# One Trainium2 core, hybrid attention block: the order of the rotary embedding on ScalarE and VectorE, its operand buffers, and the shares of the merged heads

## The reference, cut to what matters

```python
qa = rope(qa.reshape(B, S, DSW_HEADS, HEAD_DIM), positions)   # 24 window heads of 64, in 3 groups
ka = rope(ka.reshape(B, S, DSW_HEADS, HEAD_DIM), positions)
for g, (win, dil) in enumerate(zip((128, 512, 2048), (1, 4, 16))):
    o_g, lse_g = dilated_window_attention(qa[:, :, sl], ka[:, :, sl], va[:, :, sl], win, dil)
alpha = jax.nn.softmax(jnp.stack(lses), axis=0)               # shares of the 3 groups, per row and head
ya = jnp.sum(alpha[..., None] * jnp.stack(outs), axis=0)
pa = (ya * jax.nn.silu(za)) @ w_proj_a

qd, kd = rope(qd, positions), rope(kd, positions)             # 8 differential heads, 2 x 64 each
yd = differential_attention(qd, kd, vd, lam)                  # softmax 1 - lam * softmax 2, dense
yd = rms_norm(yd, diff_subln) * (1.0 - lambda_init)
pb = (yd * jax.nn.silu(zd)) @ w_proj_b
y = (sigmoid(ga) * pa + sigmoid(gb) * pb) @ w_out
return x + gate * rms_norm(y, norm_post)

def rope(x, positions):   # x1, x2: the two halves of a head
    return concatenate([x1 * cos - x2 * sin, x2 * cos + x1 * sin])
```

## Time and profile before

| | |
|---|---|
| median of 3 runs | 929.48 us (927.55 to 931.8) |
| the profiled execution's own time | 928.42 us |
| its span, first to last instruction | 926.6 us |
| mean granted TensorE clock | 0.968 of full speed |
| busy: PE, PE weight load, DVE, ACT, POOL | 834.0, 696.0, 463.1, 358.1, 494.5 us |
| DMA | 94.77 MB in 89716 packets |

### The profile page before, as it was taken

The page is one execution under the profiler, slowest core; times in us unless marked ns, Lnnn a source line. Parts: engine busy times, 40 slices in busy tenths (PEclk is TensorE's granted clock), DMA queues, the critical chain, the costliest instruction groups (busy, mean ns, idle before and its releaser), DMA issues.

```text
span 926.6 us, 12694 instructions
## 1 busy us (share of the span) xinstructions
PE 834.0 (90%) x4622; PEld 696.0 (75%) x4622; DVE 463.1 (50%) x785; ACT 358.1 (39%) x777; POOL 494.5 (53%) x657
## 2 busy tenths in 40 slices
PE   1578799999999999998988879998899999999797
PEld 1568589888878788788767757875788777888697
DVE  2866377463534344322467767757756644212122
ACT  4233344444434343423434334543545632222311
POOL 2674445353464555335767674744546537638900
PEclk9989799999989999999988999999999999999899
DMA  9763372233233323222533222222122113323421
GB/s 256 212 185 92 108 267 81 69 91 104 68 104 103 103 69 108 83 96 80 170 96 92 87 74 69 80 80 69 58 69 65 50 46 114 114 69 123 150 73 65
DMA packets 89716, 94.77 MB, mean 102 GB/s; under 512 B 5133, under 2 KB 80950, under 8 KB 89526
## 3 DMA queue, kind: packets, MB, share of 16 engines
q1 hardware_dynamic: 89360, 93.54, 33.1%
q0 software_dynamic: 240, 0.39, 0.4%
q10 hardware_dynamic: 54, 0.02, 0.0%
HBM read 78.11 MB, written 5.34 MB: 90 GB/s over the span
## 4 chain that ended last, share of the span: by engine, by line
PE 42%; POOL 17%; DVE 13%; DMA 9%; ACT 7%; issue 7%; SPq 5%; ACTq 0%; DVEq 0%; POOLq 0%
PE proj L1465 29%; POOL w_lo L671 9%; PE proj L1548 4%; DMA rope_s<-rope_x 4%; POOL rope_x L696 3%; DVE rope_o L1076 3%; SPq L551 3%; PE score L1344 2%; DMA ada<-in_w_ada 2%; PE sums L1390 2%; PE turned L1361 2%; ACT w_hi L785 1%; DVE ada_sum L1006 1%; POOL h_lo L671 1%; PE score L1319 1%
## 5 line engine op out<-in xcount | busy, mean ns | idle before, releaser
L671 POOL TENSOR_TENSOR w_lo<-raw,w_hi 128x256 fp32r<-128x256 f32 x408 | 321.7, 820 | 245.0 <-ACT w_hi L785 244.9
L1465 PE MATMUL proj<-h_hi,w_hi 128*128 128x512 f32 x608 | 255.2, 420 | 10.2 <-POOL h_lo L681 7.9
L1465 PE MATMUL proj<-h_hi,w_lo 128*128 128x512 f32 x608 | 243.5, 401 | 0.0
L1465 PE MATMUL proj<-h_lo,w_hi 128*128 128x512 f32 x608 | 243.2, 400 | 0.0
L1465 PEld LDWEIGHTS proj<-h_hi,w_hi 128*128 128x128 f32 x608 | 117.8, 194 | 46.0 <-POOL h_lo L681 9.3
L1465 PEld LDWEIGHTS proj<-h_hi,w_lo 128*128 128x128 f32 x608 | 117.7, 194 | 26.7
L1465 PEld LDWEIGHTS proj<-h_lo,w_hi 128*128 128x128 f32 x608 | 118.1, 194 | 21.4
L785 ACT ACTIVATE w_hi<-raw 128x1024 fp32r<-128x1024 f32 x102 | 106.0, 1055 | 12.8 <-PE proj L1465 7.7
L696 POOL TENSOR_TENSOR rope_x<-rope_x,cos_t 128x512 f32<-128x512 f32 x36 | 53.9, 1496 | 84.8 <-DMA rope_s<-rope_x 84.4
L1139 DVE TENSOR_TENSOR at_lo<-turned,at_hi 128x512 fp32r<-128x512 f32 x64 | 44.1, 689 | 67.5 <-ACT at_hi L887 65.2
L1390 PE MATMUL sums<-v,at_hi 128*128 128x128 f32 (+1 forms) x256 | 63.1, 316 | 14.4 <-DVE at_lo L1139 14.2
(11 more groups left out here) (236 smaller groups left out, 1545.6 us busy)
## 6 DMA issues: line engine op xcount, KB each, us to landing
raw<-in_w_in SPq DMA_DIRECT2D x88, 512.0 KB, 3.6
rope_s<-rope_x SPq DMA_DIRECT2D x144, 64.0 KB, 2.3
ada<-in_w_ada SPq DMA_DIRECT2D x16, 512.0 KB, 6.2
zd<-in_w_ada SPq DMA_DIRECT2D x8, 512.0 KB, 4.9
raw<-in_w_proj_b SPq DMA_DIRECT2D x8, 512.0 KB, 3.4
raw<-in_w_out SPq DMA_DIRECT2D x8, 512.0 KB, 3.4
rows_in<-window_rows SPq DMA_DIRECT2D x4, 792.0 KB, 4.5
window_rows<-rows_out SPq DMA_DIRECT2D x4, 528.0 KB, 4.9
```

The lines of the kernel that those rows point to most:

```text
L671: ins = nc.gpsimd.tensor_tensor(lo[:, k, :], raw[:, n % RAW, k, :], hi.bitcast(F32)[:, k, :], ALU.subtract)
L1465: ins = mm(dst, left, right, start=k == 0 and n == 0, stop=k == nk - 1 and n == 2)
```

## The change

It has four parts. (1) On ScalarE, `rope_cut` moves behind `leave_bank`, `turned_hi` and `vt_hi` of its tick, and, but for the first four tiles, one tick on, to L + 3. (2) On VectorE, the sum of the rotation is a function of its own, `rope_add`, which runs at L + 3 behind the maxima and ahead of `join` (for the first four tiles directly behind the product with sin, as before); the rest of a tile is taken at L + 4. (3) The copy and the swapped copy have two buffers each, so `rope_copy` and the swap wait for the sum of the tile before the last. (4) The maxima and denominators of all rows are loaded by four small transfers into `mix_in` at tick 96, and `merge_weights` runs once, at tick 98, for all four quarters, with 32 columns per operation for 8; `mstat` and `mix_in` lie in memory of the early tensors.

```diff
+    add_tick = lambda t: rope_tick(t) + (t.u >= 4)
+    rope_add_at = by_tick([t for t in tiles if t.kind in "qk"], add_tick)
-    rope_lo_at = by_tick([t for t in tiles if t.kind in "qk"], lambda t: rope_tick(t) + 1)
+    rope_lo_at = by_tick([t for t in tiles if t.kind in "qk"], lambda t: add_tick(t) + 1)
...
-            return (zd[:, n, :], zd[:, 4 + n, :]) if n < 4 else (rope_x[:], rope_s[:])
+            return (zd[:, n, :], zd[:, 4 + n, :]) if n < 4 else (rope_x2[:, n % 2, :], rope_s2[:, n % 2, :])
...
                 sp.wait_ge(rope_copied, n + 1)
-                if n >= 5:
-                    sp.wait_ge(rope_done, n)
+                if n >= 6:
+                    sp.wait_ge(rope_done, n - 1)
...
                     if tt:
                         sp.wait_ge(merged_done, tt)
+                    else:
+                        for i in range(NT):
+                            sp.dma_start(mix_in[:, i, :, :], scratch[:, i * P:(i + 1) * P, 4 * HD:OW].rearrange("n p f -> p n f")).then_inc(mix_in_loaded, 16)
...
                     pool.wait_ge(rows_in_loaded, 16 * (tt + 1))
-                    pool.wait_ge(shares_done, tt + 1)
+                    pool.wait_ge(shares_done, 1)
...
                 act.wait_ge(proj_done, tile.u + 1)
-                if n >= 5:
-                    act.wait_ge(rope_done, n)
+                if n >= 6:
+                    act.wait_ge(rope_done, n - 1)
...
-                for tile in rope_at(t):
-                    rope_cut(tile)
                 for tile in tiles_done(t):
                     leave_bank(tile)
                 for s in trans_at(t):
                     turned_hi(s)
                 for tile in vt_at(t):
                     vt_hi(tile)
-                for tt in mix_at(t):
-                    act.wait_ge(mix_diff, tt + 1)
-                    nc.scalar.activation(mstat[:, 32:56], mstat[:, 8:32], ACT.Exp).then_inc(mix_exp_done, 1)
+                for tile in rope_add_at(t):
+                    rope_cut(tile)
+                if t == mix_tick[0]:
+                    act.wait_ge(mix_diff, 1)
+                    nc.scalar.activation(mstat[:, 4:7, :], mstat[:, 1:4, :], ACT.Exp).then_inc(mix_exp_done, 1)
...
+            def rope_add(tile):
+                n = rope_no[tile.u]
+                at, other = rope_place(tile)
                 dve.wait_ge(rope_sin_done, n + 1)
                 dve.wait_ge(rope_cos_done, n + 1)
...
+                for tile in rope_add_at(t):
+                    if tile.u >= 4:
+                        rope_add(tile)
                 for s in scores_at(t):
                     if s.group == 3:
                         join(s)
                 for tile in rope_at(t):
                     rope_turn(tile)
+                    if tile.u < 4:
+                        rope_add(tile)
...
-                for tt in mix_at(t):
-                    merge_weights(tt)
+                if t == mix_tick[0]:
+                    merge_weights()
```

More of the change, by code:

```diff
@@ L332, in build @@
         sin_t = sb("sin_t", [P, S], on=early)
-        rope_x = sb("rope_x", [P, S], on=early)
-        rope_s = sb("rope_s", [P, S], on=early)
+        rope_x2 = sb("rope_x", [P, 2, S], on=early)
+        rope_s2 = sb("rope_s", [P, 2, S], on=early)
+        rope_x, rope_s = rope_x2[:, 0, :], rope_s2[:, 0, :]
         rope_o = sb("rope_o", [P, S], on=early)
@@ L343, in build @@
         merged = sb("merged", [P, S], on=early)
+        mstat = sb("mstat", [P, 12, 32], on=early)
+        mix_in = sb("mix_in", [P, NT, N_WIN, 8], on=early)
         early.close()
@@ L371, in build @@
         rows_in_loaded = sem("rows_in_loaded")
+        mix_in_loaded = sem("mix_in_loaded")
         x_again = [sem(f"x_again{i}") for i in range(2)]
@@ L914, in _ @@
             act.wait_ge(angle_done, 1)
-            nc.scalar.activation(sin_t[:], rope_s[:], ACT.Sin).then_inc(act_sin, 1)
+            nc.scalar.activation(sin_t[:], rope_s, ACT.Sin).then_inc(act_sin, 1)
             act.wait_ge(angle_done, 2)
@@ L1043, in _ @@
             dve.wait_ge(pos_loaded, 16)
-            link(nc.vector.tensor_copy(rope_x[:], merged[:].bitcast(I32)))
-            link(ts_(rope_x[:], rope_x[:], rope_c[:, 0:1], None, ALU.mult))
-            link(ts_(rope_o[:], rope_x[:], float(1 / (2 * np.pi)), ROUND, ALU.mult, ALU.add))
+            link(nc.vector.tensor_copy(rope_x, merged[:].bitcast(I32)))
+            link(ts_(rope_x, rope_x, rope_c[:, 0:1], None, ALU.mult))
+            link(ts_(rope_o[:], rope_x, float(1 / (2 * np.pi)), ROUND, ALU.mult, ALU.add))
             link(ts_(rope_o[:], rope_o[:], ROUND, None, ALU.subtract))
             for part in TWO_PI:
[L1049 to L1053, removed]
+                link(stt(out=rope_x, in0=rope_o[:], scalar=-part, in1=rope_x, op0=ALU.mult, op1=ALU.add))
+            link(ts_(rope_x, rope_x, PI_BELOW, -PI_BELOW, ALU.min, ALU.max))
+            ts_(rope_s, rope_x, rope_c[:, 1:2], None, ALU.mult).then_inc(angle_done, 1)
+            link(stt(out=rope_x, in0=rope_x, scalar=-1.0, in1=rope_x, op0=ALU.mult, op1=ALU.max))
+            ts_(rope_o[:], rope_x, -1.0, float(np.pi / 2), ALU.mult, ALU.add).then_inc(angle_done, 1)
             dve.wait_ge(const_done, 2)
@@ L1187, in gate_head, with merge_weights @@
                     op0=ALU.mult, op1=ALU.mult).then_inc(t_read, 1)
[L1189 to L1194, removed]
-                link(tt_(m8(0), small(0, nb), small(1, nb), ALU.min))
-                link(tt_(m8(0), m8(0), small(2, nb), ALU.min))
+            def merge_weights():
+                dve.wait_ge(mix_in_loaded, 16 * NT)
+                small = lambda g, at: mix_in[:, :, 2 * g:2 * g + 2, at:at + 4]
+                m = lambda i: mstat[:, i, :].rearrange("p (t n h) -> p t n h", t=NT, n=2)
+                link(tt_(m(0), small(0, 0), small(1, 0), ALU.min))
+                link(tt_(m(0), m(0), small(2, 0), ALU.min))
                 for g in range(3):
-                    ins = tt_(m8(8 + 8 * g), m8(0), small(g, nb), ALU.subtract)
+                    ins = tt_(m(1 + g), m(0), small(g, 0), ALU.subtract)
                 ins.then_inc(mix_diff, 1)
-                dve.wait_ge(mix_exp_done, tt + 1)
+                dve.wait_ge(mix_exp_done, 1)
                 for g in range(3):
-                    link(tt_(m8(56 + 8 * g), m8(32 + 8 * g), small(g, den), ALU.mult))
-                link(tt_(m8(80), m8(56), m8(64), ALU.add))
-                link(tt_(m8(80), m8(80), m8(72), ALU.add))
-                link(nc.vector.reciprocal(m8(80), m8(80)))
+                    link(tt_(m(7 + g), m(4 + g), small(g, 4), ALU.mult))
+                flat = lambda i: mstat[:, i, :]
+                link(tt_(flat(10), flat(7), flat(8), ALU.add))
+                link(tt_(flat(10), flat(10), flat(9), ALU.add))
+                link(nc.vector.reciprocal(flat(10), flat(10)))
                 for g in range(3):
-                    ins = tt_(m8(32 + 8 * g), m8(32 + 8 * g), m8(80), ALU.mult)
+                    ins = tt_(flat(4 + g), flat(4 + g), flat(10), ALU.mult)
                 ins.then_inc(shares_done, 1)
```

3 lines of the change are left out of this document (1 added, 2 removed).

## The result

| | before | after |
|---|---|---|
| median | 930.64 us (4 runs, 927.55 to 932.12) | 901.12 us (4 runs, 896.14 to 901.99) |
| the profiled execution's own time, and its span | 928.42, 926.6 us | 901.99, 900.2 us |
| mean granted TensorE clock | 0.968 | 0.977 |

The ratio is 0.9684, with an interval of 0.9647 to 0.9721: 3.2 % faster. The forecast was 904 us with a range of 887 to 921, so both the time and the sign held.

A forecast was written before the change was run, and what follows sets the result against it. The prediction took PE, busy 834.0 of 926.6 us, as the bound, with stalls and half-clock dips mostly in stages 6 to 8. Its terms, 3 + 1 + 4 + 4 + 4 + 8 = 24 us off 928.4, gave 904 us, range 887 to 921.

The forecast's parts named there:

- The first four tiles: Start of the kernel: ScalarE rounds v first, so PE's first scores come earlier; 3 us (0 to 5).
- Between the stages of windows: Between stages 2 and 3 a 1.54 us halt goes, PE then waits elsewhere; 3 and 4 unchanged; 1 us (-2 to 3).
- Ahead of stage 6: With two buffers a copy needs only PE's product; the 2.31 us bank wait and its dip go: 4 us (2 to 4.5).
- Stage 6 to step 42: Waits for turned probabilities go but GpSimd binds, so PE halts about 8 us with a dip; gain 4 us (-3 to 18).
- the bound of 13.6 us: Upper end for the four small transfers of part 4 holding VectorE at tick 98; the forecast took nothing.
- Stages 7 and 8: Steps 42 to 49 gain 4 us (1 to 5), steps 49 to 54 gain 8 us (4 to 10), without merges on GpSimd.
- The signs to look for: Profile after: `rope_o` waits near zero, `at_lo` and bank waits gone, longest stage 6 stall at merged rows, steps 49-54 near 42 us.
- rival C: Beside steps 33 to 54: the sum waits for GpSimd's product with cos and holds the join; slower, 942 us, chance 0.05.
- Rival B: Only the first parts pay; stages 6 to 8 give 4 instead of 16, the start 2: 917 us, chance 0.20 with small transfers.
- rival A: GpSimd is not the bound; all stalls and dips in stages 6 to 8 go: 885 us, chance 0.12.

The follow-up runs named there:

- a: The kernel before with part 4 alone (shares of the merged heads worked out once): 931.1 us, ratio 1.002.
- b: The kernel before with ScalarE's new order alone (rotated tile's rounding behind bank copies, turned probabilities and turned v), one buffer per operand: 918.3 us, ratio 0.9888.
- c: The kernel before with ScalarE's new order and two operand buffers; sum at its old tick, shares four times: 908.3 us, ratio 0.9765.
- d: The changed kernel without part 4 (shares worked out for each quarter, as before): 897.4 us, ratio 0.9662.
- f: The changed kernel without GpSimd's scaling of the merged rows by their shares: 889.0 us, ratio 0.9558.
- g: The changed kernel with the norm ahead of GpSimd's rests of weights in a tick, from tick 12 on: 902.4 us, ratio 0.9697.
- h: The changed kernel with the four merges 12 ticks earlier (ticks 86, 90, 94, 98): 896.5 us, ratio 0.9635.
- e: The changed kernel with the four small loads issued four ticks earlier (tick 92 for 96): 899.8 us, ratio 0.9668.

## Why the prediction was right, and where it was not

The sum was 3 + 1 + 4 + 4 + 4 + 8 = 24 us. Measured by the same milestones it is 2.1 + 11.2 + 4.0 - 0.5 + 1.8 + 8.1 = 26.7.

*The first four tiles: 3, measured 2.1.* The halt fell from 5.85 to 4.98 us, and the scores began at 102.53 rather than 101.4. But a, with the old order, had a halt of 4.21 us, and step 17 moves by 4 us between traces with one order. This term can't be confirmed.

*Between the stages of windows: 1, measured 11.2. This is the step that failed.* The prediction said of stages 3 and 4 that "ScalarE's waits there are not what the stored rows and the weights wait for". They are, by the chain shown above; it is worth the later sum's 4.1 us. The copy at 305.50 shows no wait of its own, since it ran right behind the rounding at 304.96, but PE's last matmul for it had ended by 301.8: it was ready and stood in the queue. And one boundary was costed where this stretch has three. The other 6.9 us came with the order and the buffers. For these the prediction counted the halt of 1.54 us between stages 2 and 3, less what would be late next, and nothing for the slow clock behind it:

```profile
265.00:277.00 12.00, 12.00 (x56) 9.82 (x54) 2.08 (x3) 5.46 (x14) 5.12 (x8) 0.72 0.42 134
```

A clock of 0.72 over 12 us is 3.4 us lost. In b, with the order alone, the clock is 1.00 at that boundary. But so it is in a, which has the old order, and whose slow stretch (0.93 from 314.7 to 366) comes later; so of the clock's share in this column a part is chance, and one trace of each kernel cannot say how much. Both stretches, with PE's busy time second and the granted clock behind the counts, in before and in after:

```profile
224.23:375.82 151.59, 146.77 (x794) 121.97 (x792) 64.09 (x78) 61.54 (x163) 77.60 (x84) 0.97 0.32 95
```
```profile
222.11:362.47 140.36, 140.36 (x794) 119.26 (x792) 64.18 (x78) 62.46 (x163) 82.24 (x85) 1.00 0.34 102
```

The same 794 matmuls: 4.8 us were idle time and 6.4 us busy time, of which the clock, from 0.97 to 1.00, accounts for about 5. All of it went, and no new wait took its place. The rest of turned v at 274.73, which was to hold PE next and left it 1.2 us at most, was late by the same chain: the maxima at that boundary, too, wait over 4 us for the stored rows.

*Ahead of stage 6: 4, measured 4.0,* but not by the buffers, as the prediction argued ("a copy needs only PE's product"). Kernel c has them and loses 1.1 us there. In c the copy's wait of 2.31 us is gone, and PE waits 2.4 us in four places for rests of weights:

```profile
428.27 0.63 ACT L824 ACTIVATE k_hi<-rope_o 128x512 fp32r<-128x512 f32 x1 [9.39 <-DVE rope_o L1077]
428.81 1.04 ACT L786 ACTIVATE w_hi<-raw 128x1024 fp32r<-128x1024 f32 x1
```

The rounding of weights is queued behind the rotation as the copy was. Only the later tick freed it (72.0 us in d, with no wait of PE); whether it needs the buffers too no run shows. The size is right by luck, the mechanism was wrong.

*Stage 6 to step 42: 4 (-3 to 18), measured -0.5.* That GpSimd's chain binds here is confirmed by f, g and h. The forecast was a halt of 8 us behind the norm's place and a dip of 4; it was 9.98 us, and PE ran at half clock behind it up to 505.2, which is 3 us lost. The size failed by 4.5 us, of which 2.6 are part 4. The prediction counted a gain for it (the waits of 1.56 and 4.82 us for the shares) and no cost; the waits did go, and the lag of the swap and the 2.35 us of slower scalings came. The small transfers did not hold VectorE, for which the bound of 13.6 us stood; they held the swap behind them. The 0.87 of the earlier trace rows was read as VectorE's time for four scalings, without asking who would be running beside them.

*Stages 7 and 8: 4 and 8, measured 1.8 and 8.1.* From 49 to 54 it took 42.7 us, near the 42 expected; but 6.9 of the 8.1 come from the order and the buffers, and 1.2 from the later sum, whose place was what the prediction named there. From 42 to 49 it is 2.2 us short of the forecast, and one stretch at half clock explains that. In after and in e, PE halts alike at the last merge, and goes on at a different clock:

```profile
538.80 1.12 PE L1378 MATMUL turned<-ident,probs 128*128 128x128 f32 x4 [2.18 <-DVE za L1226]
...
539.40:546.20 6.80, 6.80 (x22) 4.73 (x21) 4.52 (x6) 4.45 (x8) 4.62 (x6) 0.55 0.11 27
```
```profile
539.84 0.66 PE L1379 MATMUL turned<-ident,probs 128*128 128x128 f32 x4 [2.17 <-DVE za L1227]
...
541.00:548.00 7.00, 7.00 (x39) 5.71 (x36) 6.41 (x8) 3.99 (x8) 5.84 (x7) 1.00 0.27 72
```

The granted 0.55 is close to the 1.2 GHz level, 1.00 is 2.4 GHz. That column is 60.6 with the dip and 58.1 without.

*The signs to look for.* ScalarE's waits for `rope_o` were to be near zero. They fell from 152.4 us in 38 waits to

```profile
ACT k_hi L831 <- DVE rope_o L1088: 21.3, 8, 5.5
ACT q_hi L831 <- DVE rope_o L1088: 20.8, 8, 8.0
```

and from stage 6 on to 3.3 us in one wait. Near zero holds there alone. PE's waits for rests of turned probabilities were to be gone, and 4.6 of 14.2 us are left. The bank wait ahead of stage 6 and its dip are gone. The longest stall in stage 6 is where it was said to be, released by VectorE, which waits 5.52 us for the norm. VectorE's waits ahead of the sum for GpSimd did not grow, and none is for `mix_in`: rival C did not show. Rival B was wrong in stages 7 and 8 (9.9 us came) and near in stage 6, rival A needed a lighter GpSimd, and f, which has one, comes to 889 for its 885. The total was near by luck: 10 us too little in the windows met 7 us too much in stages 6 and 7.

## What to carry to other kernels

A wait on an in-order engine is charged to everything queued behind it, and from there through the other queues: before a wait is called harmless, follow it through the weights, the buffer they free, the load that needs the buffer, and whatever is queued behind that load. An operation that ran right behind a long wait says nothing about when its own input was ready. Removing a wait that kept an engine still also puts its next work beside somebody else's, so ask which critical operation then gets a neighbour. And a short halt may carry a stretch of slow clock that is longer than the halt: price both.

## What the runs showed of the hardware

VectorE's multiplication of 128x128 f32 by a column took 0.28 us as a rule (0.88 for four), 3.23 us for four beside GpSimd's scaling of rows, in after, a and e alike, and 2.76 us for four beside its rests of weights in g. The prediction knew of such a slowdown only for VectorE's instructions with two inputs in SBUF; this one has a single tensor input. (Its join of 1.88 us fell at 706.8, beside another GpSimd instruction, L740; beside the product with cos it took up to 1.87, so the reading stands.) The Trainium skill (GPSIMD Engine Reference, Key points) names, beside the instructions with two SBUF inputs, those "in a 2-port perf mode"; the trace fits that, though no row shows the mode. A halt of 2.2 us was followed by 6.8 us at 0.55 of the clock in one kernel and by none in another, so a halt's length alone does not tell what it costs. In before, a halt of 1.54 us was followed by 12 us at a mean of 0.72, which lost more than the halt did.
